# Fixed rows for the decode tokens in every expert, gathers ahead of scatter-adds, one load moved between others, a shorter end of routing, and extra matmul passes on constants

## The reference, cut to what matters

```
xn = rms_norm(x, norm1);  proj = xn @ w_in
mix = concat(sliding_window_attention(q, k, v), mamba2_ssd(z, xBC, dt))
h   = x + mix @ w_out
t   = rms_norm(h, norm2)
g   = top-1 of 4 expert groups (softmax of t @ w_grp + b_grp)
e   = top-2 of the 8 experts in that group (softmax of t @ w_exp + b_exp)
y   = h + sum over the two experts of gate * (silu(t @ w_gate[e]) * (t @ w_up[e])) @ w_down[e]
```

## Time and profile before

| what | us |
|---|---|
| median of 3 runs (lowest, highest) | 812.96 (812.08, 813.54) |
| the profiled execution | 815.63 |
| its span, first to last instruction | 813.6 |
| busy: PE, DVE, ACT, POOL | 737.7, 460.4, 273.5, 302.5 |
| mean granted TensorE clock | 0.968 of full |

### The profile page before, as it was taken

How to read it: one execution, slowest core, us unless ns; L and a number is a source line. 1 busy time by engine, 2 the same in 40 slices (tenths; PEclk the granted TensorE clock), 3 DMA queues, 4 the chain that set the end, 5 groups by cost and what they waited for, 6 DMA issues and landing times.

```text
span 813.6 us, 13104 instructions
## 1 busy us (share of the span) xinstructions
PE 737.7 (91%) x4344; PEld 533.9 (66%) x4344; DVE 460.4 (57%) x1219; ACT 273.5 (34%) x654; POOL 302.5 (37%) x365
## 2 busy tenths in 40 slices
PE   5999999999999999999959999993998888888894
PEld 2968585867777786945535553562877767767773
DVE  1679789797979797978524774655222222222221
ACT  1453544545354555355312331211222212212221
POOL 0243343423234334322000331002476566566564
PEclk9999999999999999999979999985899999999998
DMA  9900303030302901033774887112689888888842
GB/s 313 342 27 4 104 1 106 1 106 0 105 0 63 279 7 52 0 116 104 225 248 157 302 262 263 43 52 63 198 292 290 266 281 281 265 286 277 267 100 35
DMA packets 63451, 125.77 MB, mean 155 GB/s; under 512 B 20756, under 2 KB 33076, under 8 KB 63260
## 3 DMA queue, kind: packets, MB, share of 16 engines
q1 hardware_dynamic: 47252, 99.86, 36.4%
q0 software_dynamic: 13824, 16.97, 9.1%
q10 hardware_dynamic: 2336, 8.46, 2.6%
HBM read 109.83 MB, written 49.90 MB: 196 GB/s over the span
## 4 chain that ended last, share of the span: by engine, by line
issue 21%; DMA 21%; PE 19%; DVE 17%; POOL 7%; DVEq 5%; POOLq 5%; SPq 2%; ACT 2%; ACTq 0%
DMA cum_rows<-t_dram,idx_in 9%; DMA tT<-t_dram,idx_in 8%; DVE cv L1040 7%; PE bank L1732 7%; PE bank L2058 4%; PE bank L1665 3%; POOLq L1529 2%; POOL rstd L1486 2%; PE bank L2064 2%; POOLq L1485 2%; DVEq L899 2%; POOL cv L1530 2%; DMA x<-t_dram,idx_in 2%; PE bank L1756 1%; DVEq L1038 1%
## 5 line engine op out<-in xcount | busy, mean ns | idle before, releaser
L1732 PE MATMUL bank<-w_out_sb,mix_back 128*128 128x512 f32 x256 | 121.0, 617 | 8.6 <-DMA x<-in_x_prompt 8.6
L2058 PEld LDWEIGHTS bank<-w_arena 128*128 128x128 f32 x992 | 118.2, 195 | 15.6 <-issue 14.3
L2058 PE MATMUL bank<-w_arena 128*128 128x128 f32 x992 | 118.4, 279 | 0.9 <-ACT w_arena L831 0.9
L1732 PEld LDWEIGHTS bank<-w_out_sb,mix_back 128*128 128x128 f32 x256 | 47.8, 196 | 61.5 <-issue 52.5
L1484 POOL TENSOR_TENSOR stat<-stat,eps 128x1 f32<-128x1 f32 (+4 forms) x35 | 9.5, 273 | 176.5 <-ACT junk L656 103.3
L1674 PE MATMUL bank<-w_arena,tT 128*128 128x512 f32 (+1 forms) x192 | 73.3, 537 | 1.6 <-DVE tT L1024 1.6
L1674 PE MATMUL bank<-w_arena,xT 128*128 128x512 f32 (+1 forms) x192 | 71.6, 526 | 0.0
L1040 DVE SCALAR_TENSOR_TENSOR cv<-raw,par,cv 128x128 f32<-128x128 f32 x192 | 68.7, 419 | 2.4
L1427 DVE TENSOR_TENSOR w_arena<-w_arena,bank 128x128 f32<-128x128 f32 x32 | 9.2, 288 | 103.2 <-ACT w_arena L836 103.2
L2064 PE MATMUL bank<-w_arena 128*128 128x512 f32 x124 | 58.9, 597 | 0.7 <-DVE w_arena L1427 0.7
L1714 PEld LDWEIGHTS bank<-xT,w_arena 128*128 128x128 f32 x512 | 58.4, 192 | 0.5
(11 more groups left out here) (322 smaller groups left out, 1249.0 us busy)
## 6 DMA issues: line engine op xcount, KB each, us to landing
w_arena<-in_w_gate SPq DMA_DIRECT2D x31, 512.0 KB, 5.1
w_arena<-in_w_up SPq DMA_DIRECT2D x31, 512.0 KB, 7.3
w_arena<-in_w_down SPq DMA_DIRECT2D x31, 512.0 KB, 14.9
x<-in_x_prompt SPq DMA_DIRECT2D x16, 512.0 KB, 5.5
w_arena<-in_w_in SPq DMA_DIRECT2D x3, 2048.0 KB, 14.2
mix_back<-in_x_prompt_by_channel SPq DMA_DIRECT2D x8, 512.0 KB, 3.9
cum_rows<-cum_dram SPq DMA_DIRECT2D x8, 512.0 KB, 4.6
mix_dram<-mix SPq DMA_DIRECT2D x8, 512.0 KB, 5.2
```

Source lines behind the costliest of these rows:

```text
L1732: ins = pe.matmul(bank[out_bank(i, c)][:, :], mix_back[tile % 2][:, k, :], w_out[:, k, 512 * c:512 * c + 512], start=k == 0, stop=k == KC - 1)
L2058: ins = pe.matmul(out[:, a * P:(a + 1) * P], gu[:, a, k, :], xgT[w % 2][:, k, :], start=k == 0, stop=k == KC - 1)
```

## The change

There are five edits.

1. **Fixed decode slots.** An expert has 120 slots for prompt rows, and its slots 120 to 127 always hold the 8 decode tokens. Their numbers are constants, so the decode tile isn't ranked. For an expert that a decode token didn't choose, the gate is zero. The scatter-add into `y_sample` goes. Instead a tile `decoded` is loaded from `y_sample` once, DVE adds the last 32 rows of every step's result to it (`dve_decoded`), and SP stores it once at the end.
2. **Gathers ahead.** In each POOL step the gather for four steps on is issued as soon as TensorE has transposed this step's rows, ahead of the step's scatter-add.
3. **The third tile's rows between the states.** `load_next_back(2)` stands between the third and the fourth load of a decode state.
4. **Fewer steps behind the last tile.** The router uses two DVE operations where there were four. The rank is read from PSUM without a copy. For the last tile ACT and DVE each copy half of the transposed rows, gates and values are worked out ahead of the rank, and the slot table is one operation and a copy.
5. **Passes on constants.** `pe_warm(n)` issues n matmuls of the identity with 512 columns of constants, whose result nobody reads, at three places in the end of routing and five of them ahead of the first gathered tile.

```
+            for b in range(DEC):
+                if b == 3:
+                    load_next_back(2)
                 sp.dma_start(st_h[:, b], I["state_ssm"][0, b]...
...
             sp.dma_start(st_raw, I["x_sample"].rearrange("b s d -> (b s) d")).then_inc(late_in, 16)
-            load_next_back(2)
             load_first(0)
...
+            sp.dma_start(decoded[ROWS:P, :], y_sample).then_inc(dec_in, 16)
...
+            sp.wait_ge(E_["dec"], NE)
+            sp.dma_start(y_sample, decoded[ROWS:P, :]).then_inc(dec_in, 16)
...
+        def dve_turned_t(dve, i):
+            now(dve, "ttm", i)
+            last(dve, "lgm", i)
+            dve.tensor_copy(tT[:, 4:8, :], bank[6][:, :].rearrange("p (k n) -> p k n", k=4)).then_inc(T["lastT"], 1)
...
-            dve.tensor_scalar(gmask[0:n, 0, :], ..., None, ALU.is_equal)
-            dve.drain()
-            dve.tensor_scalar(gmask[0:n, 1, :], gmask[0:n, 0, :], 1.0, BIG, ALU.subtract, ALU.mult)
-            dve.tensor_tensor(le[0:n, :, :], lg..., gmask..., ALU.mult)
-            dve.drain()
-            dve.tensor_tensor(le[0:n, :, :], le[0:n, :, :], gmask..., ALU.add)
+            dve.tensor_scalar(gmask[0:n, 0, :], ..., 1.0, ALU.is_equal, ALU.subtract)
+            dve.drain()
+            dve.scalar_tensor_tensor(out=le[0:n, :, :], in0=gmask..., scalar=BIG, in1=lg..., op0=ALU.mult, op1=ALU.add)
...
             dve_routed(8)
-            dve_ranked(8)
-            dve_choices(slice(EARLY - 2, EARLY), ...)
+            dve_gates(dve, 8, P, slot_of(8))
+            dve_values(slice(EARLY - 2, EARLY), chosen[:, EARLY - 2:EARLY])
+            dve_rank(dve, 8, P, slot_of(8))
+            dve_select(slice(EARLY - 2, EARLY), row_sel[1][:, EARLY // 2 - 2:, :])
...
-            dve.tensor_scalar(slot_f[:, 0, :], bank[1][:, 0:NE], float(EMPTY), None, ALU.add)
-            dve.tensor_copy(gate_tab[:, 0:NE], bank[1][:, NE:2 * NE])
-            slot_table(0, NE).then_inc(T["slots"], 1)
+            dve.tensor_scalar(slot_tab[:, 0:NE], bank[1][:, 0:NE], con[:, C_SLOT:C_SLOT + 1], None, ALU.add)
+            dve.tensor_copy(gate_tab[:, 0:NE], bank[1][:, NE:2 * NE]).then_inc(T["slots"], 1)
...
+            def dve_decoded(j, w):
+                dve.wait_ge(E_["ya"], j + 2)
+                dve.wait_ge(E_["yd"], j + 2)
+                dve.tensor_tensor(decoded[DEC_AT:P, :], decoded[DEC_AT:P, :], yo[w][DEC_AT:P, :], ALU.add).then_inc(E_["dec"], 1)
...
             def pool_expert(group, w, left=NE):
...
+                pool.wait_ge(E_["idx"], j + 2)
+                if left > RING:
+                    pool.wait_ge(E_["turn"], j + 1)
+                    gather(xg[w], idx_in[w], e_x[w])
...
                 scatter(yo[w], w, e_out[w])
-                if left > RING:
-                    gather(xg[w], idx_in[w], e_x[w])
...
+            def pe_warm(n):
+                for _ in range(n):
+                    pe.matmul(bank[2][:, :], ident, con[:, 0:512], start=True, stop=True)
```

More of the change, by code:

```diff
@@ L287, in layer_kernel @@
         yo = [w_out[:, w, :] for w in range(RING)]
+        decoded = w_out[:, RING, :]
+        DEC_AT = P - 32
         def expert(w, group):
@@ L295, in layer_kernel @@
         idx_out = [sb(f"idx_out{w}", [P, 1], I32) for w in range(RING)]
-        idx_row = [sb(f"idx_row{w}", [P, 1], I32) for w in range(RING)]
         gate_col = [sb(f"gate_col{w}", [P, 1]) for w in range(RING)]
         loaded = sem("loaded")
+        dec_in = sem("dec_in")
         S = {}
@@ L305, in layer_kernel @@
         T = {}
-        for name in "init aneg q kT att cv dt xz scT bcT bc bx hup ch hst norm ssmT cnt part slots et over".split():
+        for name in "lastT init aneg q kT att cv dt xz scT bcT bc bx hup ch hst norm ssmT cnt part slots et over".split():
             T[name] = sem("m_" + name)
         E_ = {}
-        for name in ("turn xa xd up sil hid dn ya yd idx").split():
+        for name in ("turn xa xd up sil hid dn ready ya yd dec idx free").split():
             E_[name] = sem("e_" + name)
@@ L346, in layer_kernel, with ranked @@
         ORDER = (*range(TILES - 2), TILES, TILES - 2, TILES - 1)
+        def ranked(i):
+            return i - (i > ORDER.index(TILES))
         def width(tile):
@@ L650, in act_z, with act_square, act_turned_half, act_store_h @@
             act.activation(zs[0:n, :], bank[0][z_at:z_at + n, :], ACT.Silu).then_inc(S["z"], 1)
-        def act_residual(act, i):
+        def act_square(act, i):
+            n = width(ORDER[i])
+            now(act, "hres", i)
+            act.activation(junk[0:n, :], back(i)[0:n, :], ACT.Square, scale=D ** -0.5, accum_out=stat[0:n, 13 + i % 2:14 + i % 2]).then_inc(S["hsq"], 1)
+        def act_turned_half(act, i):
+            now(act, "ttm", i)
+            last(act, "lgm", i)
+            act.activation(tT[:, 0:4, :], bank[5][:, :].rearrange("p (k n) -> p k n", k=4), ACT.Copy).then_inc(S["tt"], 1)
+        def act_store_h(act, i):
             tile, n, h = ORDER[i], width(ORDER[i]), back(i)
@@ L979, in dve_router, with dve_gates @@
             dve.drain()
-            last(dve, "rankm", tile)
+            if n < P:
+                return
+            last(dve, "rankm", ranked(tile))
             dve.tensor_tensor(both[0:n, :], slot("onehot", n)[:, 0], slot("onehot", n)[:, 1], ALU.add).then_inc(S["rsel"], 1)
-        def dve_rank_read(dve, tile, n):
-            now(dve, "rankm", tile)
-            dve.tensor_copy(rankc[0:n, :], bank[7][0:n, 0:NE]).then_inc(S["rankd"], 1)
-        def dve_rank(dve, tile, n, slot):
+        def dve_gates(dve, tile, n, slot):
             now(dve, "gex", tile)
@@ L996, in dve_rank @@
             dve.tensor_tensor(slot("gate", n)[:, 1:2], slot("gate", n)[:, 0:1], rt[0:n, 3:4], ALU.mult)
-            dve.tensor_tensor(counted[0:n, :], counted[0:n, :], both[0:n, :], ALU.add)
-            dve.drain()
-            dve.tensor_tensor(rprod[0:n, :, :], slot("onehot", n), rankc[0:n, :].unsqueeze(1).to_broadcast([n, 2, NE]), ALU.mult)
+        def dve_rank(dve, tile, n, slot):
+            now(dve, "rankm", ranked(tile))
+            dve.tensor_tensor(rprod[0:n, :, :], slot("onehot", n), bank[7][0:n, 0:NE].unsqueeze(1).to_broadcast([n, 2, NE]), ALU.mult).then_inc(S["rankd"], 1)
             dve.drain()
             dve.tensor_reduce(slot("rank", n), rprod[0:n, :, :], AX.X, ALU.add)
+            dve.tensor_tensor(counted[0:n, :], counted[0:n, :], both[0:n, :], ALU.add)
         @block.vector
@@ L1012, in _ @@
             dve.memset(onehot[:, TILES], 0.0)
-            dve.memset(rank[:, TILES], 0.0)
             dve.memset(gate[:, TILES], 0.0)
@@ L1429, in dve_expert @@
                     dve_turned(j + 1, (w + 1) % RING)
+                if stored is not None or w > 0:
+                    dve_decoded(j - 1, (w - 1) % RING)
                 dve.wait_ge(E_["dn"], j + 2)
@@ L1753, in pe_router @@
             now(pe, "tt", tile)
-            last(pe, "rankd", tile)
+            last(pe, "rankd", ranked(tile))
             for k in range(KC):
@@ L1759, in pe_rank @@
         def pe_rank(pe, tile, n):
-            now(pe, "rsel", tile)
+            now(pe, "rsel", ranked(tile))
             pe.matmul(bank[7][0:n, 0:NE], strict[0:n, 0:n], both[0:n, :], start=True, stop=False)
```

139 lines of the change are left out of this document (76 added, 63 removed).

## The result

| | before | changed |
|---|---|---|
| median of 7 runs, us | 811.87 | 805.86 |
| lowest, highest | 810.56, 813.54 | 803.27, 807.87 |
| profiled execution, its span | 815.63, 813.6 | 805.86, 804.0 |

The account below looks back on a forecast made before the run. PE's waits were taken to bound the kernel to about 545 us, full DMA engines the experts. Terms −9.5 − 2.0 − 1.0 − 1.7 = −14.2 from 815.63 gave 801.4, or 798.8 for the median; range 785 to 807.

Parts of the forecast that it names:

- The third tile's load: PE's 8.60 us wait for `x` near 409 us goes, with half of 1.68 us of slow matmuls: −9.5 us.
- The stretch to the last h: From behind the third tile's projection to the add for the last h: no change, 0 us.
- The end of routing: From the last h to the first gather: a shorter chain brings the gather and overflow table 5.0 us earlier.
- Its halves: End of routing: −2.65 us from the last h to the add ahead of the rank, −2.4 from there to the gather.
- The term for matmuls at full clock: End of routing: rank and table matmuls at full clock, if the early passes bring it, −0.5 us (0 to −0.9).
- The passes: Five passes ahead of the first gathered tile cost +6.8 us and return −3.8 through the clock, so +3.0.
- The experts: Steps stay at 7.64 us apart from −0.10 and +0.06 a step over 26 steps: −1.0 us (−6 to +3).
- the price of the second scatter-add: Experts: removing the scatter-add into `y_sample` gains between 0 and 0.5 us a step, taken as 0.10.
- the sign that the prediction had set for itself: The prediction would be wrong above all if the expert step moved by more than 0.2 us.
- The slower rival: Experts: gathers ahead delay weight tiles, the step grows by 0.5 us or more, 815 us at 8.2 a step; 4%.
- The end: Behind the last expert step: the last scatter-add into `y_sample` goes, −1.7 us (−1.0 to −1.85).
- a late load: Third tile: `x` lands at 414.6, so the edit gives 2.8 us instead of 9.5: 805.5 us; 12%.

Follow-up runs that it names:

- before_swap: The kernel before with two blocks of slots exchanged (ranks 32 to 63 and 64 to 95 trade partitions), nothing else; 788.05 us, ratio 0.9719.
- load_moved: The kernel before with only the third tile's load moved between the third and fourth state; 804.38 us, ratio 0.9908.
- before_ahead: The kernel before with only the gathers moved ahead of the scatter-adds, and the wait for a free result buffer one slot earlier; 806.72 us, ratio 0.9942.
- one_scatter: The kernel before without its second scatter-add, the one into the decode output; 818.70 us, ratio 1.0086.
- pool_pause_2: The changed kernel with about 1.8 us of unneeded POOL work behind each scatter-add, without a drain; 804.81 us, ratio 0.9913.
- the spread kernels: The changed kernel with prompt ranks spread over the slots: 764.34 us with all passes on constants, 762.47 without the last five, 761.25 without any.
- empty_free: The changed kernel with a second scatter-add per step whose rows all fall outside the target and which nothing in the steps waits for; 795.87 us, ratio 0.9794.

## Why the prediction was wrong

- **The third tile's load** was right in mechanism and near in size: −10.45 for −9.5, since all of the 1.68 us of slow matmuls came back and not half. The landing time was met by two misses that cancel, as said above.
- **The stretch to the last h** was put at nothing and gave −4.43. Before, it held two stretches of low clock, 0.67 from 494 to 499 us and 0.69 from 533.3 to 538.7; in the changed kernel both places have 1.00. `before_swap`, whose edit only renumbers slots, has no low clock in this part and takes 117.6 us for it, where the kernel before takes 120.84 and the changed one 116.41. So some 3.2 us are clock and 1.2 the shorter code. The low clock goes with the code for the most part: `load_moved`, `before_ahead` and `one_scatter`, which have the old code there, take 120.8 to 120.9 as well, and the profiles with the changed code all take 116.4 but `pool_pause_2` (118.1). Why the clock falls there is open.
- **The end of routing** was right: −5.1 for −5.0. Its halves fit too: from the last h to the add ahead of the rank −2.56 for −2.65, and from there to the gather −2.54 for −2.4. The agreement to a tenth is partly luck, for the four other profiles with the old code there take 16.9 to 17.5 us and not 17.97. The term for matmuls at full clock, −0.5, is what the early passes bring in the spread kernels, 0.50.
- **The passes** were right: 6.78 us for 6.8, and 2.75 in sum for 3.0. They were forecast to cost more than they return, and leaving them out bears that out.
- **The experts** are the step that failed: "I take −0.10 and +0.06 a step, 26 steps until the weights end: −1.0". That the earlier gather changes nothing held in the changed kernel (234.0 us with the old place, 235.0 with the new); in the kernel before it gave 3.7 us. Its reason, that half of the engines were full, held. But it was never "some 20 us earlier": POOL reaches it only behind the scatter-add of the step before, at 628.07 for one of them, and its old place, behind the next scatter-add, would have been at 634.3. The term that failed is another: the price of the second scatter-add was bounded "between 0 and 0.5 us a step" of gain, as if taking requests out of a full queue could only help. Taking it out cost 7.9 us in the kernel before (`one_scatter`), and putting an empty one back won about 11 in the changed one. The steps grew by 0.31 us in the mean, against the sign that the prediction had set for itself, 0.2. The prediction counted no clock in the experts either, and the loss here is the clock behind long waits, with the sum of the waits as before. The slower rival named the late weight tile; its cause, the gathers' order, was not it.
- **The end** was right: −1.5 for −1.7.

That 805.86 lies inside the stated range of 785 to 807 is luck: the upper end was held for a late load, and the load was not late.

With the experts at the even 7.6 that `empty_free` has, 221.8 in place of 235.0 us, the profiled execution would have been 792.7; all the other steps together came to −19.3 where −13.2 was forecast, and 3.2 of that difference of 6.1 are the two stretches of low clock. 3.6 us of the −9.6 stand in the profiles alone: the medians differ by 6.0, and the profile of before is slower than all of its runs in the table. The experts don't hold them, for `load_moved` repeats their 225.3 us with 225.2. Some may stand at the end of routing and from there to the first down matmul, where the four other profiles with the old code are shorter by 0.5 to 1.1 and by 0.4 to 1.0; the rest is open.

## What to carry to other kernels

A mean DMA share of 0.86 that alternates between 1.0 and 0.5 can mean that half of the engines are full; which partitions the rows of a gather fall on is then worth more than when it is issued. Taking work out of a shared queue can make a steady wait of 1.3 us a step into long ones that cost TensorE's clock as well: look at the longest wait, not the sum. Passes that are to keep the clock up need idle time that nothing waits behind; here the last five stood on the path.

## What the runs showed of the hardware that wasn't expected

- 128 scatter requests a step that all fall outside their target, and change no row, shortened 31 steps from 235.0 to 221.8 us, while a gather took 20.9 us to land in place of 10.3.
- PE was idle for the same sum over the 31 steps (28.1 and 27.9 us), and still they took 9.65 us more where single waits reached 3.8 us: the granted clock fell to 0.69 behind one of 3.56, and stayed at 1.00 where no wait was over 1.3.
- POOL stood idle for about 5 us a step behind a drain that follows an indirect scatter-add, and not without the drain.
- With the rows spread over the partitions the same transfers went at 338 GB/s, against 271 in the changed kernel.
